# Last block's input and up projections with the weights held and the tokens moving; index heads and selection rounds further up in the block

## The reference, cut to what matters

```python
def second_block(x, c, w_ada, b_ada, g_mix, w_in, b_in, rel_bias, ...):
    mod = silu(c) @ w_ada + b_ada                       # sh1, sc1, ga1, sh2, sc2, ga2
    xn = rms_norm(h, g_mix) * (1 + sc1) + sh1
    proj = xn @ w_in + b_in                             # 1024 x 5448
    q, k, v, qi, ki, wi, xr, yr, gate_a, gate_b = split(proj)
    # attention: score = sum_h wi * relu(qi_h . ki), the 64 best keys of each query, softmax over them
    attn = dsa_attention(q, k, v, qi, ki, wi, rel_bias)
    xr = causal_dwconv(xr, conv_rnn_w, conv_rnn_b)      # 4 taps along the tokens
    rnn = rg_lru(xr, ...) * gelu(yr)                    # two gates, then a scan along the tokens
    merged = sigmoid(gate_a) * (attn @ w_o_attn) + sigmoid(gate_b) * (rnn @ w_o_rnn)
    h = h + ga1 * (merged @ w_out)
    xn = rms_norm(h, g_ffn) * (1 + sc2) + sh2
    up = causal_dwconv(xn @ w_up, conv_ffn_w, conv_ffn_b)   # 1024 x 5632, 3 taps
    val, gte = split(up)
    h = h + ga2 * ((silu(gte) * val) @ w_down)
    return rms_norm(h, g_final)
```

## Time and profile before

| | |
|---|---|
| median of three runs | 1084.53 us (1083.74 to 1086.95) |
| the profiled execution | 1086.36 us, span 1084.3 us |
| mean granted TensorE clock | 0.982 of 2.4 GHz |
| PE busy | 1026.4 us, 95% of the span |
| DVE busy | 732.6 us, 68% |
| ACT busy | 585.8 us, 54% |
| POOL busy | 115.6 us, 11% |
| chain that ended last, by engine | PE 73%, DVE 11%, ACT 8%, issue 4% |

### The profile page before, as it was taken

One profiled execution on the slowest core, in us unless ns is written; L12 is line 12 of the kernel. 1 busy time (PEld: TensorE's weight loads), 2 busy tenths in 40 slices (PEclk: granted clock), 3 DMA queues, 4 the chain that ended last, 5 costly groups with the idle time before them and its releaser, 6 DMA issues.

```text
span 1084.3 us, 13459 instructions
## 1 busy us (share of the span) xinstructions
PE 1026.4 (95%) x5180; PEld 850.1 (78%) x5180; DVE 732.6 (68%) x986; ACT 585.8 (54%) x842; POOL 115.6 (11%) x168
## 2 busy tenths in 40 slices
PE   6897999999999989899999999997999999999996
PEld 4675878889888777788888878886877788888885
DVE  5567775566346577578888666769766765777753
ACT  6657554444335567544443354577656456676641
POOL 0112140000000022200000011013630000000001
PEclk9999999999999999999999989999999999999998
DMA  9765479555556432389999796535465535554431
GB/s 348 274 170 73 136 202 303 188 181 174 194 175 197 157 113 76 101 287 352 353 325 320 295 317 215 166 121 165 147 213 206 163 112 184 191 193 156 175 136 39
DMA packets 98190, 213.98 MB, mean 197 GB/s; under 512 B 5440, under 2 KB 12880, under 8 KB 94736
## 3 DMA queue, kind: packets, MB, share of 16 engines
q1 hardware_dynamic: 93424, 196.39, 53.2%
q0 software_dynamic: 4416, 16.51, 6.3%
q10 hardware_dynamic: 288, 0.23, 0.1%
HBM read 208.39 MB, written 6.15 MB: 198 GB/s over the span
## 4 chain that ended last, share of the span: by engine, by line
PE 73%; DVE 11%; ACT 8%; issue 4%; DMA 2%; POOL 1%; SPq 0%; DVEq 0%; ACTq 0%; POOLq 0%
PE bank L883 22%; PE bank L885 22%; PE bank L884 22%; ACT hi L1199 4%; DVE lo L1634 4%; PE bank L861 3%; PE bank L898 1%; PE bank L863 1%; ACT junk L1062 1%; DMA raw<-in_w_in_a 1%; DVE early L1465 1%; DVE xres L1508 1%; DMA raw<-in_w_gate_up 1%; DMA early<-in_memT 1%; PE bank L944 0%
## 5 line engine op out<-in xcount | busy, mean ns | idle before, releaser
L1634 DVE TENSOR_TENSOR lo<-raw,hi 128x2048 fp32r<-128x2048 f32 (+1 forms) x164 | 366.9, 2240 | 215.7 <-ACT hi L1199 215.1
L1199 ACT ACTIVATE hi<-raw 128x2048 fp32r<-128x2048 f32 (+1 forms) x164 | 303.7, 1855 | 184.2 <-PE bank L885 144.0
L883 PE MATMUL bank<-hi,xTh 128*128 128x512 f32 (+2 forms) x896 | 346.8, 387 | 2.6 <-DVE lo L1634 2.2
L885 PE MATMUL bank<-hi,xTl 128*128 128x512 f32 (+2 forms) x896 | 337.7, 377 | 0.0
L884 PE MATMUL bank<-lo,xTh 128*128 128x512 f32 (+2 forms) x896 | 337.7, 377 | 0.0
L883 PEld LDWEIGHTS bank<-hi,xTh 128*128 128x128 f32 x896 | 170.6, 190 | 33.7 <-DVE lo L1634 2.8
L885 PEld LDWEIGHTS bank<-hi,xTl 128*128 128x128 f32 x896 | 170.2, 190 | 31.7
L884 PEld LDWEIGHTS bank<-lo,xTh 128*128 128x128 f32 x896 | 170.5, 190 | 28.5
L883 PE MATMUL bank<-hi,hTh 128*128 128x512 f32 x264 | 103.5, 392 | 0.2 <-DVE lo L1634 0.2
L885 PE MATMUL bank<-hi,hTl 128*128 128x512 f32 x264 | 102.8, 389 | 0.0
L884 PE MATMUL bank<-lo,hTh 128*128 128x512 f32 x264 | 102.8, 389 | 0.0
(11 more groups left out here) (346 smaller groups left out, 1315.2 us busy)
## 6 DMA issues: line engine op xcount, KB each, us to landing
raw<-in_w_gate_up SPq DMA_DIRECT2D x44, 1024.0 KB, 6.4
raw<-in_w_down SPq DMA_DIRECT2D x30, 1024.0 KB, 5.1
raw<-in_w_ada SPq DMA_DIRECT2D x24, 1024.0 KB, 6.2
raw<-in_w_up SPq DMA_DIRECT2D x22, 1024.0 KB, 5.1
raw<-in_w_in SPq DMA_DIRECT2D x21, 1024.0 KB, 5.0
raw<-in_w_out SPq DMA_DIRECT2D x12, 1024.0 KB, 5.1
raw<-in_w_in_b SPq DMA_DIRECT2D x10, 1024.0 KB, 5.1
raw<-in_w_in_a SPq DMA_DIRECT2D x6, 1024.0 KB, 11.9
```

Of the source, the lines that this page charges most:

```text
L883: e.matmul(o, sh, h[:, k, :], start=p.first and k == 0, stop=False)
L885: done = e.matmul(o, sl, h[:, k, :], start=False, stop=p.last and k == p.nk - 1)
L1199: e.activation(hi_s[m % SPLITS][:, 0:n], raw[p.at % RAWS][:, 0:n], ACT.Copy).then_inc(hi_made, 1)
L1634: e.tensor_tensor(lo_s[s][:, 0:n], raw[p.at % RAWS][:, 0:n], hi_s[s][:, 0:n].bitcast(F), ALU.subtract).then_inc(lo_made, 1)
```

## The change

The columns of `qi`, `q`, `xr`, `yr` and the whole up projection are computed in 256-column tiles of kind `across` or `raw`, each of one part. TensorE now holds 128x128 blocks of the weights and moves all 256 tokens past them, so that the result stands with the columns on the partitions, in one bank, where the consumer reads it. The staging copies and the transposes of these columns go. The bias of `qi`, `q` and `xr`, before a row added by DVE, is added by ACT inside the PSUM bank, two instructions to a step (`with_bias`); that of `yr` was in the GELU's instruction already. The steps of `IN2` are rearranged: index heads start half a tile after their keys, the selection rounds are spread over `xr`, `yr` and `q`, ending before `kv`, and the last gap of the stage is empty.

```diff
-IN2 = [("qi", 768, 512, ["", "", ""]),
-       ("kw", 1280, 72, ["qi0", "qi2", "x1"]),
-       ("xr", 1352, 512, ["ki", "h0", ""]),
-       ("yr", 2376, 512, ["conv00", "h2 conv02", "h4"]),
-       ("xr", 1864, 512, ["gelu00", "gelu02 h6", "gate000 gate002 top"]),
-       ("yr", 2888, 512, ["gate010 gate012 top0", "conv10 top1", "rec0"]),
-       ("q", 0, 512, ["conv12 top2", "gelu10 inc0 top3", "gelu12 scan0"]),
-       ("kv", 512, 256, ["top4", "half0 bias0 q0 gate100 top5", "q2 gate102 gate110 gate112"]),
-       ("gb", 4424, 512, ["kv top6 top7", "rec1 mask", "attend inc1 s0"]),
+IN2 = [("qi", 768, 512, ["", "", "qi0"]),
+       ("kw", 1280, 72, ["qi2", "", "x1"]),
+       ("xr", 1352, 512, ["ki", "h0", "h2 conv00"]),
+       ("yr", 2376, 512, ["h4", "conv02 h6", "top"]),
+       ("xr", 1864, 512, ["gelu00 top0", "gelu02 top1", "top2 gate000 gate002"]),
+       ("yr", 2888, 512, ["gate010 gate012 conv10 top3", "top4", "rec0 top5"]),
+       ("q", 0, 512, ["conv12 top6", "gelu10 inc0 top7", "gelu12 scan0 mask"]),
+       ("kv", 512, 256, ["q0", "half0 bias0 gate100", "q2 gate102 gate110 gate112"]),
+       ("gb", 4424, 512, ["kv attend", "rec1", "inc1 s0"]),
        ("gb", 4936, 512, ["s1 scan1", "s2", "half1 bias1"]),
-       ("ga", 3400, 512, ["", "s3", "s4"]),
-       ("ga", 3912, 512, ["s5", "s6", "s7"])]
+       ("ga", 3400, 512, ["s3", "s4", "s5"]),
+       ("ga", 3912, 512, ["s6", "s7", ""])]
...
-UP2 = tiles_of(DFF)[-1:] + tiles_of(DFF)[:-1]
+UP2 = [(c, 256) for c in [2560] + list(range(0, 2560, 256))]
...
-        elif kind == "conv":
-            self.turn(task, ON_D)
-        elif kind in ("gelu", "rgate"):
+        elif kind == "conv":
+            self.empty(task, ON_D)
+        elif kind == "gelu":
+            self.empty(task, ON_A)
+        elif kind == "rgate":
             self.turn(task, ON_A)
...
+            self.linear("across", what, c, 256, 1, ("z", 0), 0, between[0:1])
+            for name in between[1].split():
+                self.named(name)
+            self.linear("across", what, c + 256, 256, 1, ("z", 0), 0, between[2:3])
...
-                self.linear("raw", what, c, w, 2 if w == 512 else 1, ("z", 1))
+                self.linear("raw", what, c, w, 1, ("z", 1))
...
+            def across(p, ch, h, lo, xh, xl):
+
+                if ch == 0:
+                    await_bank(e, p.tile.bank)
+                o, at = x_bank(p.tile.bank)[:, ch * 256:ch * 256 + 256], slice(ch * 128, ch * 128 + 128)
+                for k in range(8):
+                    if (p.source, k) not in seen:
+                        seen.add((p.source, k))
+                        e.wait_ge(*ready(p.source, k))
+                    e.matmul(o, h[:, k, at], xh[:, k, :], start=k == 0, stop=False)
+                    e.matmul(o, lo[:, k, at], xh[:, k, :], start=False, stop=False)
+                    done = e.matmul(o, h[:, k, at], xl[:, k, :], start=False, stop=k == 7)
+                done.then_inc(part_done if ch else acc_first, 1)
...
-                elif kind in ("qi", "q"):
-                    e.wait_ge(acc_dve, order.tile_of["in2", kind, 768 if kind == "qi" else 0].d1)
-                    turned(claim(step), blocks_of(staged2_slot(kind), name[0] * 128, 2))
...
-                elif kind == "raw":
-                    n = t_.j - order.tile_of["raw", "gate", UP2[0][0]].j
-                    if n >= 2:
-                        was = tiles[t_.j - 2]
-                        e.wait_ge(x_full, filled(("cv", was.c, was.l, was.w // 128 - 2)))
-                    for t in range(2):
-                        e.wait_ge(*full[t])
-                        e.activation(nrm_halves[n % 2][:, t, 0:w], pair[t][:, 0:w], ACT.Copy).then_inc(acc_act, 1)
...
+            def with_bias(name, columns):
+
+                e.wait_ge(*summed(name))
+                for j in range(2):
+                    x = x_bank(name)[:, j * 256:(j + 1) * 256]
+                    e.activation(x, x, ACT.Identity, bias=columns[:, j:j + 1]).then_inc(on_act, 1)
+                    n = own.up()
+                e.wait_ge(on_act, n)
+
...
                 elif kind == "conv":
                     half, k = name
-                    e.wait_ge(x_full, filled(step))
+                    with_bias(step, bias_xr[:, 4 * half + k:4 * half + k + 2])
```

More of the change, by code:

```diff
@@ L120, in __init__ @@
         self.chunks = (2 * nk + 3) // 4
+        if tile.bank:
+            self.chunks = 2
 class AccTile:
@@ L350, in tile @@
         self.tile_of[kind, l, c] = t
+        if t.bank:
+            self.take(t.bank)
+            self.summed_by[t.bank] = t
+            return t
         for half in range(2):
@@ L371, in part @@
             tile.m = m
+            if tile.bank:
+                self.turn_at[tile.bank] = (None, None, None)
     def evacuate(self, t):
@@ L379, in evacuate @@
                 self.need(task)
+        if t.bank:
+            if t.kind == "raw":
+                self.later.append(t.bank)
+            return
         self.steps.append(("evac", t.j))
```

102 lines of the change are left out of this document (40 added, 62 removed).

## The result

Median 1093.47 us (1092.18 to 1095.58, four runs) against 1084.13 us (1083.51 to 1086.95, four runs) of the kernel before in the same job: ratio 1.0079, 95% interval 1.0055 to 1.0102. Forecast were 1077.1 us and, with 0.09, a loss. The profiled execution took 1093.7 us, span 1091.7 at a mean clock of 0.982 of 2.4 GHz (before 1086.36, 1084.3, 0.982).

The account below looks back on a forecast made before the run. TensorE, busy for 95% of the span, was taken to bound the kernel. Up projection -3.9 and input projection -3.5 sum to -7.4 us, from 1084.5 to 1077.1 us; range 1068 to 1083.5.

Parts of the forecast that it names:

- The up projection, -3.9 us: Up projection: 20 parts turned 256 wide add 5.8 us, 22 groups of transposes that go save 9.7 us.
- weight-load rival: Up projection: weight loads no longer overlap, so narrow matmuls stand 0.130 us apart; +15 us, 1092 us; chance 0.09.
- A rule against it: All narrow matmuls: by a documented issue distance they cost 24 us, less 15 for the transposes, so +9 us.
- The stage as a whole: Input projection with its attention steps: -3.5 us in sum, of which 1.8 is TensorE's own work.
- What is then ahead are the rounds and the mask ... ends about 784.4, -4.7 us.: Input projection: earlier mask brings second scan and scores 4 to 5 us sooner; the wait at 789.08 ends about 784.4.
- ACT's own walk: Input projection: ACT's order walked with row durations; done with `q0` at about 740.8, then waiting for POOL's product.
- But this attention step stands one chunk ... further up, so that chunk is still to be done: -2.0.: Input projection: a 2.7 us chunk remains behind the moved attention step, leaving -2.0 of the -4.7 us.
- I let 1.5 of the 1.82 us wait at 815.14 go.: Last attention wait: the stage's empty last gap gives the next heads 2.7 us, so 1.5 us of waiting goes.
- `half0` starts at about 742.3.: Input projection, ACT: `half0` starts 1.5 us sooner than 743.82; a start at 738 or 745 would make the forecast wrong.
- The wait moved from `q0` to `kv`: Input projection, TensorE: no wait at `q0`, some 7 us at `kv` ending about 753.6, clock loss +1.5 us behind it.
- The bias pairs: Input projection, ACT: eight added pairs of bias instructions at 1.2 us each, 9.6 us in all.
- ACT takes the stage over: Input projection: dear bias pairs or late gates and `q2` keep `kv` late; stage 0 to +3, say 1082 us; chance 0.21.

Follow-up runs that it names:

- e1: Kernel before with only the up projection of the change, table of columns unwidened: 1081.95 us, ratio 0.9967 to the kernel before.
- e2: Kernel before with sixteen unused columns in the table and the index weights' buffer put into the small table: 1091.18 us, ratio 1.0048 to the kernel before.
- e3: The changed kernel with four statistics buffers packed, so the large buffers behind lie where they lay before: 1087.35 us, ratio 1.0019 to the kernel before.
- e4: The changed kernel with `attend` put back behind `rec1`, in the gap of `inc1`: 1093.22 us, ratio 1.0064 to the kernel before.
- e7: e3 with a round in place of the mask behind the scan, and mask, `gate112` and `attend` later: 1083.56 us, ratio 0.9984 to the kernel before.
- e12: e1 with the steps `s3` to `s7` one gap further up: 1086.40 us, ratio 1.0006 to the kernel before.
- e6: e1, input projection still staged, with the change's step places (`qi`, `conv` steps one gap later than there): 1086.05 us, ratio 1.0008 to the kernel before.
- e9: e1 with rounds, mask and index heads at the change's places, `attend` and `s` steps as before: 1084.04 us, ratio 0.9976 to the kernel before.
- e13: e5 with the round `top4` behind the scan and `q0` ahead of `half0`: 1081.26 us, ratio 0.9962 to the kernel before.
- e5: e3 with every step of `IN2` back in its old gap, input projection still without staging: 1084.70 us, ratio 0.9994 to the kernel before.

## Why the prediction was wrong, step by step

- **The up projection, -3.9 us.** Right: -3.3 in the profile, -3.6 alone (e1). The weight-load rival, the only slower one, fell: the distance is 0.120 us. Its 1092 us, and the 9 us that the prediction works out under "A rule against it", lie near the measured time (+8.6 us by the ratio) by chance, since both put the loss into the narrow matmuls. The loss came by ways that no rival had.
- **The table's sixteen columns.** The prediction had no term for them. They cost 5.2 us alone (e2) and 6.5 inside the change (e3 against it): the largest single item, and shown by both. Had it been priced, the forecast would still have been 10 us off.
- **The stage as a whole** was forecast at -3.5 us and took +5.5: 9.0 us off. Of these the next step is 6.3, the last attention wait 1.5, and 1.2 are left over.
- **"What is then ahead are the rounds and the mask ... ends about 784.4, -4.7 us."** This is the step that failed in the input projection. It walked ACT and DVE and let POOL follow. The wait ended at 790.67, 1.6 us later than before and not 4.7 sooner. ACT's own walk was right: it was through with `q0` at 741.27 on the clock of before (forecast 740.8) and then stood idle for POOL for 5.30 us. Two things in POOL's queue held it up. Its product behind the scan stood still for DVE's split (5.15 us in place of 2.35), and `attend`'s adds, with their transfer, stood ahead of `rec1` (product at 759.47 on the clock of before, not 752.67). `attend` put back by itself did nothing for the end of the wait (790.73, e4), since the copies and the transposes then came late. With both repaired, and a gate moved, it ended at 787.90 (e7). Why it isn't 784.4 even then stays open.
- **"But this attention step stands one chunk ... further up, so that chunk is still to be done: -2.0."** The chunk of 2.7 us was taken as a deduction from a gain of 4.7. There was no gain, and moving these steps up is a loss by itself: 4.2 us (e12), wait and clock together. e6 minus e9 gives 3.5 for it and `attend`; the share of `attend` alone is below what these runs can tell (e4: 1.6).
- **"I let 1.5 of the 1.82 us wait at 815.14 go."** It stayed at 1.77 us, and at 1.81 in e3, e6, e7 and e12, which all have the empty gap behind it.
- **"`half0` starts at about 742.3."** 746.57 on the clock of before, beyond the 745 that the prediction named as its sign of being wrong. The rounds and the staging, both taken away, had let POOL into SBUF ahead of the split. Put back a round and it is repaired: e7 and e13.
- **The wait moved from `q0` to `kv`.** Right, with length, end (1.1 us late) and clock: 759 to 764 had 0.68. The bias pairs cost 0.81 us, not 1.2, so ACT had more room than forecast, and the rival "ACT takes the stage over" fell as the cause of the late waits: the places cost in e6 too, where ACT has no bias pair.
- **The start of the stage** had no term: 1.9 us of waits for `z` where there were none. e5 and e13 have 0.80 of them (0.65 and 0.15), with the clock at half speed there, so that they can be a part of the 2.9 us that e5 loses to e1.

By the ratios the loss divides along one chain of kernels, whose steps sum to the whole by construction: up projection -3.6 (e1), staging-free input projection +2.9 (e5 against e1), new places +2.7 (e3 against e5), buffers' place +6.5 (the change against e3), in all +8.5 of 8.6. The places come to 2.7 or 4.5 (e6 against e1), and the difference is inside the uncertainty. The change's parts without its places and the table, with two steps set anew, are good for -0.38% (e13), against -0.33% for the up projection alone: these two can't be told apart, so whether the input projection without staging gains anything stays open.

## What to carry to other kernels

Walk every engine's queue for a moved step, the idlest too: POOL was 11% busy, and TensorE's longest waits hung on its order and on its meetings with DVE. Before an operation is removed, look at what slipped in beside it on the engine next door. And when a table grows, compare the distance between starts in stretches that the change doesn't touch: if they moved, the buffers' place did it, and packing something small puts it back.

## What was not expected of the hardware

The place of buffers in SBUF changes a matmul's distance by up to 3% (0.2267 to 0.2334 us for 32 or 64 bytes), in streams whose instructions are the same; 256-wide matmuls out of a buffer that did not move kept 0.120. A DVE and a POOL instruction with two inputs in SBUF each take turns, one of them waiting in full: 5.15 against 2.35 us on POOL, 3.05 against 0.42 on DVE; and DVE's copies from SBUF to SBUF, with one input, took 2.25 against 0.63 us beside POOL's adds. And the clock behind the same 72-wide matmuls cost 0 to 3.4 us from one profiled execution to the next, so that single stretches compare only once that is taken off.
